# A memory pair moved to the end of the step loop, with the output projection between its steps

## The reference, cut to what matters

```python
h = rms_norm(x, g_in[layer]);  proj = h @ w_in[layer]
oA = dilated_mixture_attention(qA, kA, vA, slopes_a)      # 8 heads, causal, 1024 keys
oB = dsa_attention(qB, kB, vB, qI, kI, wI, slopes_b)      # 4 heads, top 256 keys of each query
oM = memory_attention(qM, kM, vM)                         # 4 heads, 256 memory tokens
o = jnp.concatenate([oA, oB, oM], axis=-1) * jax.nn.silu(gate)
x = rms_norm(x + o @ w_out[layer], g_final)
```

## Time and profile before

| | us |
|---|---|
| three runs, median (lowest, highest) | 764.49 (759.87, 768.49) |
| the profiled execution's own time | 761.14 |
| its span in the profile | 759.3 |
| PE busy | 690.5 (91%) |
| DVE / ACT / POOL busy | 438.9 / 331.6 / 131.5 |

### The profile page before, as it was taken

One profiled execution on the slowest core, in us unless ns is written; L12 is line 12 of the kernel. 1 busy time (PEld: TensorE's weight loads), 2 busy tenths in 40 slices (PEclk: granted clock), 3 DMA queues, 4 the chain that ended last, 5 costly groups with the idle time before them and its releaser, 6 DMA issues.

```text
span 759.3 us, 11469 instructions
## 1 busy us (share of the span) xinstructions
PE 690.5 (91%) x4229; PEld 543.4 (72%) x4229; DVE 438.9 (58%) x1012; ACT 331.6 (44%) x633; POOL 131.5 (17%) x94
## 2 busy tenths in 40 slices
PE   1878999899999999999999999998979967899995
PEld 1667788676777777777777777776767745678884
DVE  4956775356564486648765975498734456222433
ACT  3666665334353345424443544354635356131411
POOL 1111100101220231131114111411140024011320
PEclk9999999989999999999999999999999997999999
DMA  8421112101111221211121112111120027104231
GB/s 298 106 56 28 28 28 83 29 0 42 43 28 43 98 57 43 66 45 44 43 84 41 31 42 84 42 30 42 28 70 20 25 73 252 41 29 155 106 111 56
DMA packets 53176, 48.76 MB, mean 64 GB/s; under 512 B 5745, under 2 KB 45697, under 8 KB 53121
## 3 DMA queue, kind: packets, MB, share of 16 engines
q1 hardware_dynamic: 53120, 48.02, 20.6%
HBM read 40.15 MB, written 7.86 MB: 63 GB/s over the span
## 4 chain that ended last, share of the span: by engine, by line
PE 79%; DVE 8%; issue 4%; ACT 4%; DMA 2%; POOL 2%; SPq 0%; DVEq 0%; ACTq 0%; POOLq 0%
PE j_ps L1268 23%; PE s_ps L1268 10%; PE o_ps L1403 8%; PE pt_ps L1379 8%; PE j_ps L1450 6%; PE s_ps L1450 6%; PE s_ps L1304 5%; PE o_ps L1268 3%; PE s_ps L1323 3%; PE pt_ps L1323 2%; DVE picked L1033 2%; PE pt_ps L1425 1%; POOL w_hl L578 1%; PE j_ps L1244 1%; DVE probT L1116 1%
## 5 line engine op out<-in xcount | busy, mean ns | idle before, releaser
L1268 PE MATMUL j_ps<-h_hi,w_hl 128*128 128x512 f32 (+2 forms) x624 | 203.2, 391 | 0.9 <-issue 0.9
L1268 PEld LDWEIGHTS j_ps<-h_hi,w_hl 128*128 128x128 f32 (+1 forms) x624 | 115.7, 186 | 24.7 <-issue 1.5
L578 POOL TENSOR_TENSOR w_hl<-w_raw,w_hl 128x1024 fp32r<-128x1024 f32 (+1 forms) x30 | 70.8, 2360 | 355.0 <-ACT w_hl L671 355.0
L1268 PE MATMUL j_ps<-h_lo,w_hl 128*128 128x512 f32 (+2 forms) x312 | 119.3, 382 | 0.0
L825 ACT ACTIVATE prob<-prob,nmax 128x256 f32<-128x256 f32 (+7 forms) x128 | 89.9, 703 | 41.2 <-DVE nmax L1107 36.8
L813 ACT ACTIVATE probT<-pt_ps 128x512 f32<-128x512 f32 (+3 forms) x88 | 41.3, 469 | 151.8 <-PE pt_ps L1379 151.2
L1379 PE MATMUL pt_ps<-ident,prob 128*128 128x128 f32 x496 | 76.0, 289 | 7.3 <-DVE gate L1134 6.7
L1268 PE MATMUL s_ps<-h_hi,w_hl 128*128 128x512 f32 x240 | 79.9, 402 | 1.1 <-POOL w_hl L578 1.1
L1379 PEld LDWEIGHTS pt_ps<-ident,prob 128*128 128x128 f32 x496 | 54.8, 144 | 28.4 <-issue 24.6
L1033 DVE TENSOR_SCALAR_CACHE_REDUCE picked<-idx,tk 128x384 f32<-128x384 f32 (+5 forms) x72 | 67.9, 943 | 1.6
L1268 PEld LDWEIGHTS j_ps<-h_lo,w_hl 128*128 128x128 f32 (+1 forms) x312 | 58.4, 187 | 10.7
(11 more groups left out here) (213 smaller groups left out, 1060.4 us busy)
## 6 DMA issues: line engine op xcount, KB each, us to landing
w_raw<-in_w_in_dram SPq DMA_DIRECT2D x28, 512.0 KB, 4.0
bias<-in_a_tab_dram SPq DMA_DIRECT2D x8, 512.0 KB, 5.0
mixed_scratch<-gate SPq DMA_DIRECT2D x14, 256.0 KB, 2.2
bias<-mixed_scratch SPq DMA_DIRECT2D x8, 448.0 KB, 4.7
bias<-in_w_out_dram SPq DMA_DIRECT2D x6, 512.0 KB, 3.7
idx<-in_x_dram SPq DMA_DIRECT2D x4, 512.0 KB, 5.6
probT<-in_w_mem_kv_dram SPq DMA_DIRECT2D x4, 512.0 KB, 6.1
prob<-in_x_dram SPq DMA_DIRECT2D x4, 512.0 KB, 4.4
```

What stands on the lines that cost most here:

```text
L578: pool.tensor_tensor(w_hl[:, w % 2, 1, :, 0:n], w_raw[:, :, 0:n], w_hl[:, w % 2, 0, :, 0:n].bitcast(F32), ALU.subtract).then_inc(w_lo_read ...
L1268: last = pe.matmul(bank[0:n, at:], a[:, k, 0:n], c[:, k, HALF * b + at:HALF * b + HALF], start=(k == 0 and q == 0), stop=(k == KD - 1 and ...
```

## The change

The order of the pairs becomes M0, A0 to A3, B0, B1, M1. All that hangs on the place of a pair moves with it:

- M0 now precedes an A pair and carries eight fills. A3 carries six (steps 4 and 5 are bare), B0 six (the gate of M1 comes in its steps 4 and 5), and B1 four: its own gate and the q of M1, in steps 0, 1, 3 and 5.
- Tile 2's choice stays in M0, tiles 3 to 6 are chosen in A0 to A3, and tile 7's in B0, in a shorter plan of its own (`LAST_COUNTS`: slots 0 to 16 in steps 1 to 5). It is settled in step 6 of B0; step 7 of B0 reads its mask.
- The chunks of `w_out` are split in steps 2 to 7 of B1, one in each of steps 2 to 5 and two in each of 6 and 7, with five rooms for the raw chunks.
- The 15 units up to tile 3's first half run in step 0 (one unit) and steps 1 to 7 (two each) of M1, the 16th behind it. The order of tiles is 4, 5, 6, 7, 0, 1, 2, 3. For tiles 4 to 7 the unit leaves out pair M1 (21 matmuls instead of 24), and four groups of six matmuls at the very end (`project_last`) add it.
- The outputs of B1 and M1 are split in SBUF in halves of 512 tokens (`part_hi` on ACT, `part_lo` on POOL) and do not go through DRAM.
- Tiles 0 and 1 get their final norm in the last step of M1; tiles 2 to 5 and then 6 and 7 get theirs after the last matmul.
- Memory scores use the three-pass hi/lo product (six matmuls of 64x256) instead of one full-precision pass, so q and k of the memory pairs get a low part on DVE.
- Some `tensor_tensor` operations on DVE, that of the odd chunks' low part among them, become `scalar_tensor_tensor` with the same operands.

The core of the diff:

```diff
-PAIRS = [("M", 0, 6), ("M", 1, 7), ("A", 0, 0), ("A", 1, 1), ("A", 2, 2), ("A", 3, 3), ("B", 0, 4), ("B", 1, 5)]
+PAIRS = [("M", 0, 6), ("A", 0, 0), ("A", 1, 1), ("A", 2, 2), ("A", 3, 3), ("B", 0, 4), ("B", 1, 5), ("M", 1, 7)]
...
+Q_SLOT = [0] * (NP - 1) + [2]
...
+ENDING = {0: (("gate", NP - 2), 0), 1: (("q", NP - 1), 0), 3: (("gate", NP - 2), 1), 5: (("q", NP - 1), 1)}
...
-WO_PER_STEP = [3, 2, 2, 1]
...
-EARLY_OUT = {STEPS - 3: (None, (0, 0), None), STEPS - 2: ((0, 1), (1, 0), None),
-             STEPS - 1: ((1, 1), (2, 0), None), STEPS: ((2, 1), (3, 0), (3, 1))}
+WO_AT = {STEPS - NT - 6: [0], STEPS - NT - 5: [1], STEPS - NT - 4: [2], STEPS - NT - 3: [3],
+         STEPS - NT - 2: [4, 5], STEPS - NT - 1: [6, 7]}
+WO_ROOM = [0, 1, 2, 3, 4, 0, 1, 2]
+MIXED_ROOM = [3, 2]
+OUT_TILES = [4, 5, 6, 7, 0, 1, 2, 3]
+OUT_UNITS = [(t, b) for t in OUT_TILES for b in range(2)]
+LATE = [4, 5, 6, 7]
+FILL_OUT = {STEPS - 8: (None, None, (4, 0)), STEPS: (None, None, (3, 1))}
+for _n in range(7):
+    FILL_OUT[STEPS - 7 + _n] = (OUT_UNITS[2 * _n + 1], None, OUT_UNITS[2 * _n + 2])
+LENT_OUT = [u for u in OUT_UNITS if u[1] == 0]
+FINAL_ORDER = [0, 1, 2, 3, 4, 5, 6, 7]
+MIX_AT = {STEPS - NT - 1: [0], STEPS - NT: [1], STEPS - 7: [2], STEPS - 6: [3],
+          STEPS - 5: [4], STEPS - 4: [5], STEPS - 3: [6], STEPS - 2: [7]}
+PART_AT = {STEPS - NT - 3: (NP - 2, 0), STEPS - NT: (NP - 2, 1), STEPS - 4: (NP - 1, 0), STEPS: (NP - 1, 1)}
+PARTS = list(PART_AT.values())
+PART_SLOT = {NP - 2: 6, NP - 1: 4}
...
+LAST_COUNTS = [2, 2, 2, 2, 2, 1, 2, 1, 2, 1, 0, 0, 0, 0]
+def settled_at(p, i):
+    if i == 0 and 1 <= p < len(IDX_TILES):
+        return p - 1
+    return len(IDX_TILES) - 1 if (p, i) == (len(IDX_TILES) - 1, NT - 2) else None
...
+                if at == 0:
                     load_wo(0)
                     load_wo(1)
-                if last >= 0:
-
-                    for n in wo_of_step(s):
-                        if WO_ROOMS <= n + WO_ROOMS - 1 < NP:
-                            load_wo(n + WO_ROOMS - 1)
-                if last == 4:
+                if at == 1:
+                    load_wo(2)
+                    load_wo(3)
+                if at == 2:
+                    load_wo(4)
+                if at in (3, 4, 5):
+                    load_wo(at + 2)
+                if at == NT - 2:
+                    load_mixed(0)
+                if at == NT - 1:
+                    load_mixed(1)
+                if at == NT:
+                    for a in range(2):
+                        sp.wait_ge(biased[a], s)
+                    for t in (4, 5, 6, 7, 0):
+                        load_residual(t)
                     for b in range(2):
                         sp.wait_ge(wo_lo_ready[b], NP // 2)
-                        load_mixed(b)
-                    for g in range(2):
-                        sp.wait_ge(og_stored[g], 16 * (NP - 1))
...
-                elif PAIRS[p][0] == "A":
-                    last = part(qk[both, 1, cut], both, qk[both, 0, cut], query_scale(p, 0))
+                elif PAIRS[p][0] != "B":
+                    hi, lo = qk[:, Q_SLOT[p], cut], qk[:, Q_SLOT[p] + 1, cut]
+                    last = part(lo, both, hi, query_scale(p, 0))
                 else:
...
+                if s == STEPS - 1:
+                    square_row(0)
+                    square_row(1)
+                    y_root(0, 0, 2)
...
-                    dve.tensor_tensor(wo_lo[:, n, :], wo_raw[n % WO_ROOMS],
-                                      wo_hi[:, n, :].bitcast(F32), ALU.subtract).then_inc(wo_lo_ready[1], 1)
+                    dve.scalar_tensor_tensor(out=wo_chunk(wo_lo, n), scalar=1.0,
+                                             in0=wo_raw[WO_ROOM[n]].rearrange("p (b c) -> p b c", b=2),
+                                             in1=wo_chunk(wo_hi, n).bitcast(F32), op0=ALU.mult,
+                                             op1=ALU.subtract).then_inc(wo_lo_ready[1], 1)
...
+                if s == STEPS - 1:
+                    norm_rows(0, 0, 2)
...
+            for n in range(len(LATE)):
+                add_last(n)
+            norm_rows(1, 2, 6)
+            norm_rows(2, 6, 8)
...
-                    last = []
-                    for a in range(2):
-                        rows = slice(DH * a, DH * a + DH)
-                        last += [pe.matmul(s_ps[a][:, 0:N_MEM], q_m[rows, P * i:P * i + P], k_m[rows, PAIRS[p][1], :],
-                                           start=True, stop=True)]
+                    hi, lo = (km[:, PAIRS[p][1], n, :] for n in range(2))
...
+                for p in range(NP - 2):
                     for q, (a, c) in enumerate(passes):
-                        last = pe.matmul(bank, a[:, p, :], c[:, p, cut],
-                                         start=(p == 0 and q == 0), stop=(p == NP - 1 and q == 2))
+                        pe.matmul(bank, a[:, p, :], wo_half(c, p, b), start=(p == 0 and q == 0), stop=False)
+                pairs = [NP - 2] + ([] if t in LATE else [NP - 1])
+                for p in pairs:
+                    pe.wait_ge(part_lo_ready, PARTS.index((p, t // 4)) + 1)
+                    for q, (a, c) in enumerate(parts_of(p, t, b)):
...
+            def project_last(n):
+                t = LATE[n]
+                if n == 0:
+                    pe.wait_ge(part_lo_ready, len(PARTS))
+                    for a in range(2):
+                        pe.wait_ge(biased[a], STEPS)
+                if n >= 2:
+                    pe.wait_ge(last_added, n - 1)
+                for b in range(2):
+                    for q, (a, c) in enumerate(parts_of(NP - 1, t, b)):
+                        last = pe.matmul(s_ps[n % 2][:, HALF * b:HALF * b + HALF], a, c, start=(q == 0), stop=(q == 2))
+                last.then_inc(out_done, 1)
```

402 lines of the change are left out of this document (212 added, 190 removed).

## The result

Four runs of the changed kernel gave 775.66 us as median (774.08 to 777.83), four of the kernel before beside them 763.67. The ratio is 1.0155, with a 95% interval of 1.0114 to 1.0197: slower, as forecast (776.5). The profiled execution took 775.92 us with a span of 774.1; the span before was 759.3.

What follows compares the result with a forecast made beforehand. PE was taken to set the pace, with waits on DVE and ACT where steps lack fills. Stretches summed to 768.3, plus 3 us of low clock 771.3; with 5.2 from span to median, 776.5 us (1.6% slower), range 764 to 788.

Steps and rivals of the forecast that it cites:

- A3: Pair A3 with six fills: 63.9 us plus 8.0 of waits for DVE's choice slots in bare steps, 71.9.
- B0: Pair B0 with six fills: 70.1 us, less 2.2 of old waits, plus 5.9 for tile 7's choice, 73.8.
- B1: Pair B1 with four fills: 53.0 us plus 9.6 of waits from the chunks of `w_out`, 62.6.
- low clock: After the two longest waits, A3's bare steps and the opening of M1: 3 us added to the span.
- M0, A0 to A2: Stretches with all their fills: 60.0 us for M0, 222.0 for A0 to A2.
- waits from tile 7's slots: In B0, four places where DVE comes late, by 1.3, 1.0, 2.9 and 0.7 us: 5.9 more.
- the rival of the late mask: Step 7 of B0 waits for POOL's mask, PE stands 5.3 to 12 us: 783 to 790 us, chance 0.10.
- the 2.1 us for step 4: In B1's bare step 4, a copy behind ACT's chunk, then DVE's, loses 2.1 us.
- Steps 6 and 7: Bare steps of B1 with two output chunks each: 6.3 us of waits on the two together.
- Opening of M1: First memory step before its unit: 5.2 us of PE's work plus helpers' work and hand-overs, 11.0.
- The memory steps: In M1, fifteen units at 76.7 us plus the steps' own scores, turns and values at 12.9.
- The last step and the end: Last memory step 11.6 us, with 4.5 of DVE work before the copy; end 20.3, 14.5 of it uncovered.

Runs made afterwards that it cites:

- Run 3: The changed kernel with 19 matmuls of no use added to PE in the waits of A3's bare steps 4 and 5: 776.6 us, ratio 1.0186.
- run 6: The changed kernel with B1's output chunks divided otherwise: DVE low parts 0 to 3, POOL 4 to 7, ACT's high parts 0 to 3 before evacuation: 772.4 us, ratio 1.0094.
- run 5: The changed kernel with the choice slots of tiles 2 to 7 following each other without regard to pairs, none in A3's bare steps: 781.9 us, ratio 1.0198.
- Runs 2: The changed kernel with tile 6's choice slots moved out of A3's bare steps 4 and 5: 777.8 us, ratio 1.0167.
- 9: The changed kernel with tile 7's choice slots later in B0, 3, 3, 3, 2 and 6 in steps 1 to 5: 779.7 us, ratio 1.0207.
- Run 4: The changed kernel with its end reordered: last projections before unit (3, 1), only tile 3 left behind the last matmul: 769.2 us, ratio 1.0075.

## Why the prediction was right, step by step

The forecast was made of stretches, and they can be compared one by one:

| stretch | before | forecast | after |
|---|---|---|---|
| start of the steps | 145.5 | 145.5 | 146.4 |
| M0 | 44.5 | 60.0 | 59.4 |
| M1 in second place | 61.8 | | |
| A0 to A2 | 222.7 | 222.0 | 221.9 |
| A3 | 77.5 | 71.9 | 74.5 |
| B0 | 59.1 | 73.8 | 72.8 |
| B1 | 75.9 | 62.6 | 66.0 |
| from there to the end | 72.3 | 132.5 | 133.1 |
| low clock, in one sum | | 3.0 | in the rows |
| span | 759.3 | 771.3 | 774.1 |

- **M0, A0 to A2:** within 0.6 and 0.1 us. A stretch with all its fills costs PE's work and little else: PE is idle 0.88 and 2.44 us there.
- **A3:** the waits were forecast as 8.0, and PE is idle 8.37. What was missing is the clock: PE is busy 66.17 where A2's work less two fills is 74.16 - 10.94 = 63.22. That is 2.95 us for A3 alone, where I had 3 for the whole kernel. Run 3 got 2.0 of them back. So the low clock was mis-sized: with 1.6 us in B1 (below) and 0.8 in M1's first step (PE busy 11.42, and 10.66 at a clock of 1.00 in run 6) it cost 5.4 in these three stretches.
- **B0:** the waits from tile 7's slots were forecast at 1.3, 1.0, 2.9 and 0.7; the trace has 1.35, 0.95, 2.85 and none. The prediction shows no working for these four, so how close they are is not to be counted as a result of its method; the idle time of B0 in all was forecast at 10.1 and is 9.20. The mask was ready at 564.8 and asked for at 566.5, so the rival of the late mask stayed away by 1.7 us. That an all-reduce can begin late and PE pays for it is shown by run 5 in A2, with a wait of 4.26 us.
- **B1:** too small by 3.4 us. The largest miss is the 2.1 us for step 4, which measured 3.70: I had counted ACT's chunk but not the silu of the gate in the same list; before, no gate was filled in B1. ACT and DVE ahead of that wait, in the changed kernel:

```profile
603.35 0.60 ACT L789 ACTIVATE gate<-j_ps 128x512 f32<-128x512 f32 x1 [3.88 <-PE j_ps L1365]
603.97 1.28 ACT L797 ACT_TABLE_LOAD   x1
605.26 1.06 ACT L797 ACTIVATE gate<-gate 128x1024 f32<-128x1024 f32 x1
606.22 1.04 ACT L939 ACTIVATE h_hi<-bias 128x1024 fp32r<-128x1024 f32 x1
607.17 0.58 ACT L899 ACTIVATE probT<-pt_ps 128x512 f32<-128x512 f32 x1
607.30 1.23 DVE L1289 SCALAR_TENSOR_TENSOR h_lo<-bias,h_hi 128x1024 fp32r<-128x1024 f32 x1 [8.43 <-ACT h_hi L939]
607.76 1.28 ACT L911 ACT_TABLE_LOAD   x1
609.18 0.69 DVE L1198 COPY probT<-pt_ps 128x512 f32<-128x512 f32 x1
```

A table load of 1.28 us and the silu's 1.06 stand ahead of the chunk's high part, for which DVE waits 8.43 us; its low part, a bias and the copy follow. The second table load comes behind ACT's copy and delays none of these. The low clock adds about 1.6 (53.93 against 74.16 - 4 x 5.47 = 52.28). Steps 6 and 7 were forecast at 6.3 and have waits of 1.78, 0.61, 3.70 and 0.74, 6.8 in sum.

- **Opening of M1:** too large. With its unit I had 15.8 us and it took 14.10, with 2.7 us idle and not some 5 in one piece. The sum put ACT's and DVE's work behind PE's 5.2 us, and they overlap: DVE's chunk ran from 641.75 to 644.30 and PE's turns from 641.97 to 643.94. Runs 2, 3 and 9 had 17.8 with the same idle time.
- **The memory steps:** too small. For the rest of M1 up to unit (3, 0) I had 84.8 us (76.7 + 12.9 less the first unit) and it took 86.4. With units of 4.8 and 5.47 us a step's own work comes to 2.0 us and not 1.75; the figure of 2.2 that the sum started from was nearer. This and the opening nearly cancel.
- **The last step and the end:** the wait was forecast at 4.5 and is 4.39. Behind the last matmul I had 14.5 and it is 14.1 (7.6 before). Run 4 shows that it is DVE's norms that stand there: in another order it is 9.7.
- **A reading:** the prediction's first paragraph gives clocks of 1.00 to 0.98 for M1, A2 and A3; the rows have 1.00 for all three. Nothing hangs on it.
- **The chunk's low part:** DVE's new form takes 2.55 us beside POOL and 1.23 alone, as the old one took 2.97 and 1.23. The rule of the Trainium skill, "SBUF — State Buffer", section "Who interferes with whom", agrees with the trace here.

So the added idle time is of three parts: 10.8 us more idle time in the end stretch than in the tail before, 7.1 in A3 and B0, 1.9 in B1 with the opening, against 5.3 less in the memory pairs; the rest, some 2 us less, lies in the start and in A0 to A2, and PE's work is 2.3 us longer. The new order of pairs does not force the slowdown: with DVE's and ACT's work put where it is covered, it is 1.1 to 1.4% faster than the kernel before. That is no gain of the order alone, since no run gave the old order a better plan of its slots and chunks or useless matmuls. Nor did a run take out the six-matmul scores or the low parts of the memory pairs; the steps that hold them show no idle time that could be theirs.

That the time came out within 1 us was luck in part. The span was forecast 2.8 us too low, and the 5.2 us added from span to median were 3.6 too many, since the median of the changed kernel lies only 1.6 above its span.

What stays open is what decides when the lower clock comes with a wait and how long it stays. The traces show it behind some waits of 1.8 to 4.4 us and not behind others. Which ones they are differs between the profiled executions, and since the executions of one kernel differ in mean clock as well, no run tells an effect of an edit apart from what one execution does anyway.

## What to carry to other kernels

A plan that moves covering work must be read for what it uncovers on the helper engines: for each step without cover, add up what stands in their lists ahead of the operation that the main engine waits for, table loads and the late start of an all-reduce included. Such a sum came within 0.4 us of A3's waits here (8.0 for 8.37) and missed by 1.6 where an item of the list was forgotten. A wait is to be priced higher than its length where the clock falls behind it (2.95 us beside 8.37 in A3). Measure by stretches, since a gain at one place can be hidden by the clock at another, and compare a stretch with the same stretch in several traces before an effect of 1 or 2 us is believed.

## What the runs showed of the hardware

POOL's all-reduce began 8.52 us after a tensor operation when its input was ready, and 0.1 us after its flag when POOL had been idle 17.57 us; the first mask operation behind tile 7's all-reduce took 7.81 us to begin in the kernel before, 7.63 in the changed one and 6.74 in run 9. So this time runs ahead of the wait for the flag, and a long idle time hides it. The Trainium skill, "GPSIMD Engine Reference", section "2.1 Instruction dispatch", has about 6 us for the first call of a freshly loaded kernel; the rows named here are above it, and one start in run 5's trace, at 189.01, is below it with 5.71.

Useless matmuls in waits made two stretches shorter: A3 by 2.04 us with 19 of them, and B1 by 2.75 with 16 (1.3 to 2.8 against five traces). A set of ACT's tables took 1.28 us to load; the Trainium skill, "ScalarE: Activation LUTs", section "What ACT_TABLE_LOAD costs", has about 1.28 us too, and a drain of 1.38 on top of it. The rows of B1 above show no drain: the operation ahead ends at 603.95, the load begins at 603.97 and the silu at 605.26.
